# Sample residual tiles: high and low input halves side by side in one 512-column product

## The reference, cut to what matters

```python
x = x + y.astype(x.dtype)                      # y = mixer output @ ev_w_out or od_w_out
x = x + cross_attention(h, m, ...)             # ends in o @ x_w_o
x = x + (jnp.square(jax.nn.relu(h @ p['mlp_w1'][layer])) @ p['mlp_w2'][layer]).astype(x.dtype)
```

## Time and profile before

| | |
|---|---|
| Median of three runs | 2537.8 us (2537.19 to 2540.1) |
| The profiled execution: its own time, its span | 2539.81 us, 2538.0 us |
| PE busy | 2443.0 us, 96% of the span |
| DVE busy | 1531.7 us, 60% |
| ACT busy | 1150.5 us, 45% |
| Mean granted PE clock | 0.986 of full speed |

### The profile page before, as it was taken

The page is one execution under the profiler, slowest core; times in us unless marked ns, Lnnn a source line. Parts: engine busy times, 40 slices in busy tenths (PEclk is TensorE's granted clock), DMA queues, the critical chain, the costliest instruction groups (busy, mean ns, idle before and its releaser), DMA issues.

```text
span 2538.0 us, 35247 instructions
## 1 busy us (share of the span) xinstructions
PE 2443.0 (96%) x14102; PEld 2075.0 (82%) x14102; DVE 1531.7 (60%) x2599; ACT 1150.5 (45%) x2010; POOL 0.2 (0%) x4
## 2 busy tenths in 40 slices
PE   7997799899999999999999999999999999999999
PEld 4887576778888999899778888778788888888887
DVE  8988756767546755564565446656886645533332
ACT  4232336344433555544454444445665443423422
POOL 0000000000000000000000000000000000000000
PEclk9998899999999999999999999999999999999999
DMA  5324532255312455444224323223334423433332
GB/s 189 95 67 103 167 111 96 80 169 191 108 59 85 156 183 184 123 132 136 78 73 157 116 81 119 75 84 101 92 92 142 132 73 88 141 99 100 92 100 91
DMA packets 109667, 289.24 MB, mean 114 GB/s; under 512 B 18913, under 2 KB 41569, under 8 KB 108225
## 3 DMA queue, kind: packets, MB, share of 16 engines
q1 hardware_dynamic: 101392, 261.36, 33.5%
q10 hardware_dynamic: 8112, 25.63, 3.1%
HBM read 265.35 MB, written 19.50 MB: 112 GB/s over the span
## 4 chain that ended last, share of the span: by engine, by line
PE 81%; DVE 12%; ACT 4%; issue 2%; DMA 1%; SPq 0%; ACTq 0%; DVEq 0%
PE ps L1414 65%; PE ps L1504 2%; PE ps L338 2%; PE ps L1479 2%; PE ps L334 2%; DVE wlo L1391 1%; PE ps L1522 1%; PE ps L1546 1%; DVE ps L1697 1%; DVE ps L1696 1%; DVE yP L1698 1%; ACT yP L1565 1%; DMA wraw<-wt 1%; DVE x L555 1%; PE ps L1446 1%
## 5 line engine op out<-in xcount | busy, mean ns | idle before, releaser
L1414 PE MATMUL ps<-in_hP,whi 128*128 128x512 f32 x1336 | 541.1, 405 | 1.6 <-issue 1.6
L1386 ACT ACTIVATE whi<-wraw 128x1024 fp32r<-128x1024 f32 x430 | 452.2, 1053 | 194.1 <-PE ps L1414 128.7
L1391 DVE TENSOR_TENSOR wlo<-wraw,whi 128x1024 fp32r<-128x1024 f32 x431 | 523.4, 1218 | 22.7 <-ACT whi L1386 22.4
L1414 PE MATMUL ps<-in_hP,wlo 128*128 128x512 f32 x1336 | 522.9, 391 | 0.0
L1414 PE MATMUL ps<-in_lP,whi 128*128 128x512 f32 x1336 | 522.1, 391 | 0.0
L1414 PE MATMUL ps<-in_hS,whi 128*128 128x256 f32 x1088 | 320.0, 294 | 5.6 <-DVE x L1719 4.3
L1414 PE MATMUL ps<-in_lS,whi 128*128 128x256 f32 x1088 | 309.4, 284 | 0.0
L1414 PE MATMUL ps<-in_hS,wlo 128*128 128x256 f32 x1088 | 309.3, 284 | 0.0
L1414 PEld LDWEIGHTS ps<-in_hP,whi 128*128 128x128 f32 x1336 | 252.4, 189 | 63.1 <-issue 11.0
L1414 PEld LDWEIGHTS ps<-in_lP,whi 128*128 128x128 f32 x1336 | 252.3, 189 | 55.5 <-issue 5.0
L1414 PEld LDWEIGHTS ps<-in_hP,wlo 128*128 128x128 f32 x1336 | 251.9, 189 | 54.2
(11 more groups left out here) (471 smaller groups left out, 3685.7 us busy)
## 6 DMA issues: line engine op xcount, KB each, us to landing
wraw<-wt SPq DMA_DIRECT2D x432, 512.0 KB, 3.5
wraw<-wt ACTq DMA_DIRECT2D x17, 512.0 KB, 4.1
k_scratch<-region_P SPq DMA_DIRECT2D x16, 256.0 KB, 3.1
v_scratch<-vtmp SPq DMA_DIRECT2D x32, 128.0 KB, 3.0
x<-x_in SPq DMA_DIRECT2D x4, 768.0 KB, 6.8
mix_u<-x SPq DMA_DIRECT2D x32, 64.0 KB, 3.4
mix_mem<-mem_in ACTq DMA_DIRECT2D x4, 512.0 KB, 6.5
x<-x_in ACTq DMA_DIRECT2D x1, 2048.0 KB, 12.7
```

Of the source, the lines that this page charges most:

```text
L1386: nc.scalar.activation(whi[:, (n + 3) % NHI, :, :], wraw[:, ws(n), :, :], ACT.Copy).then_inc(wh.sem, 1)
L1391: nc.vector.tensor_tensor(wlo[:, ws(n), :, :], wraw[:, ws(n), :, :], whi[:, (n + 3) % NHI, :, :].bitcast(F32), ALU.subtract).then_inc(wr.s ...
L1414: last = nc.tensor.matmul(ps[:, m % 2, 0:N[prod.g]], w_[:, k, :], x_[:, k, :], start=(k == 0 and j == 0), stop=(k == KT - 1 and j == 2))
```

## The change

For residual tiles of the sample alone the high and low halves of the input are laid side by side in memory (`hid_S`, `in_S`), as `[high 256 | low 256]` for each k. One matmul of 512 columns under w_h makes w_h·x_h in columns 0 to 255 of the bank and w_h·x_l in columns 256 to 511. The product w_l·x_h stays at 256 columns and adds to the first half. So a tile has 16 matmuls and 16 weight loads where it had 24. The two halves of the bank are then added to `x` one after the other, by two DVE instructions with a `dve_chain` between them. Prompt tiles and the sample's other products are as they were.

```diff
-                hid_h[g] = sb(f"hid_h{g}", [P, KT, N[g]], F32R, on=over)
-                hid_l[g] = sb(f"hid_l{g}", [P, KT, N[g]], F32R, on=over)
+                if g == "S":
+                    hid_S = sb("hid_S", [P, KT, 2, TS], F32R, on=over)
+                    hid_h[g], hid_l[g] = hid_S[:, :, 0, :], hid_S[:, :, 1, :]
...
+            in_S = sb("in_S", [P, KT, 2, TS], F32R, on=fl)
...
+                    self.pair = None if (kind, g) != ("res", "S") else in_S if rhs is None else hid_S
...
                     if i == 0 and prod.ready is not None:
                         pe.wait_ge(*prod.ready(k))
+                    if prod.pair is not None:
+                        both = prod.pair[:, k, :, :].rearrange("p z n -> p (z n)")
+                        if k < KT - 1:
+                            nc.tensor.matmul(ps[:, m % 2, :], w_h[:, k, :], both, start=(k == 0), stop=False)
+                        last = nc.tensor.matmul(ps[:, m % 2, 0:TS], w_l[:, k, :], h_[:, k, :], start=False, stop=False)
+                        if k == KT - 1:
+                            last = nc.tensor.matmul(ps[:, m % 2, :], w_h[:, k, :], both, start=False, stop=True)
+                        continue
...
                     v.wait_ge(td.sem, m + 1)
+                    if prod.pair is not None:
+                        dve_chain(nc.vector.tensor_tensor(x[:, i, cols(g)], ps[:, b, TS:2 * TS], x[:, i, cols(g)], ALU.add))
                     nc.vector.tensor_tensor(x[:, i, cols(g)], ps[:, b, 0:N[g]], x[:, i, cols(g)], ALU.add).then_inc(tf[b].sem, 1)
```

More of the change, by code:

```diff
@@ L918, in trunk_tail @@
                 over = ExitStack()
-                hid_h[g] = sb(f"hid_h{g}", [P, KT, N[g]], F32R, on=over)
-                hid_l[g] = sb(f"hid_l{g}", [P, KT, N[g]], F32R, on=over)
+                if g == "S":
+                    hid_S = sb("hid_S", [P, KT, 2, TS], F32R, on=over)
+                    hid_h[g], hid_l[g] = hid_S[:, :, 0, :], hid_S[:, :, 1, :]
+                else:
+                    hid_h[g] = sb(f"hid_h{g}", [P, KT, N[g]], F32R, on=over)
+                    hid_l[g] = sb(f"hid_l{g}", [P, KT, N[g]], F32R, on=over)
                 over.close()
@@ L926, in trunk_tail @@
             over.close()
-            in_h = {"P": in_hP, "S": sb("in_hS", [P, KT, TS], F32R, on=fl)}
-            in_l = {"P": in_lP, "S": sb("in_lS", [P, KT, TS], F32R, on=fl)}
+            in_S = sb("in_S", [P, KT, 2, TS], F32R, on=fl)
+            in_h = {"P": in_hP, "S": in_S[:, :, 0, :]}
+            in_l = {"P": in_lP, "S": in_S[:, :, 1, :]}
             ring = {g: sb(f"ring{g}", [P, 2, N[g]], on=fl) for g in "PS"}
@@ L1111, in __init__ @@
                     self.kind, self.g, self.w0, self.ready, self.n, self.layer = "mem", "P", WT[f"kv{layer}"], ready, 2 * KT, layer
-                    self.rhs, self.norm, self.up = (in_h["P"], in_l["P"]), None, None
+                    self.rhs, self.norm, self.up, self.pair = (in_h["P"], in_l["P"]), None, None, None
                     self.sq, self.kad, self.ksc = z["sqd"].take(KT), z["kad"].take(XH), z["ksc"].take(XH)
```

## The result

The changed kernel takes 2542.5 us in the median of nine runs (2540.6 to 2548.1), the kernel before 2538.1 us in nine runs on the same chip (2535.2 to 2540.1). The ratio is 1.0022, with a 95% interval of 1.0012 to 1.0032: about 5.6 us slower, between 3.0 and 8.1 (the two medians themselves are 4.4 us apart). It is a small loss, and the interval doesn't reach down to 1.

The account below looks back on a forecast made before the run. PE bounds the kernel with 81% of the chain, DVE leading in short stretches; -4.5 + 2.15 + 2.15 + 2.7 + 0.3 + 0 = +2.8, rounded to +2.7, on 2537.8 gives 2540.5 us, range 2534.5 to 2546.

Parts of the forecast that it names:

- if a mixed pair of matmuls takes anything but 0.347 us: Sign that the prediction is wrong: a 512- and a 256-column matmul together should take 0.227 and 0.120 us.
- the other: Sign that the prediction is wrong: attention rounds of 23.1 us grow or shrink by over 0.3 us.
- The price of the second add: On DVE, each sample tile's second add costs 0.47 us, between 0.34 and about 0.6; 45 us in total.
- The rival of 0.34 us: Second add costs only 0.34 us on DVE: paced stretches cost 4.9 in all, total +0.4, 2538.2 us; chance 0.09.
- 5 x 0.47 - 0.2: Cross output of layer 1: five second adds paid in full, less two shorter tiles, +2.15 us; last 8 tiles the same.
- the second adds of tiles 0 and 1 lie in the wait for it: Cross output of layer 1: the first two tiles' second adds are hidden while DVE's statistic is awaited.
- I take the middle: On PE, a sample tile shortens by 0.106 us to 2.774 us, between bounds of no saving and 0.21 us.
- if the missing fixed part came back at the change of width: Bound on PE's gain: the sample tile would stay at 2.88 us; as a rival 2545 us, chance 0.08.
- Cross output of layer 0: Beside the prompt's cross attention DVE has 1.41 us in each slot, so 8 x 0.106 = 0.85 us is gained.
- Attention output of layer 1: Eight tiles with room on DVE but a late weight tile: an estimated gain of 0.3 us.
- Attention of MLP 1: 16 tiles beside the differential attention: DVE becomes full, PE's gain is lost, net 0, between -1.7 and +7.5 us.
- the rival of broken margins: DVE's thin cover in MLP 0 and the attention rounds fails: +5 to +10, 2543 to 2548 us; chance 0.17.

Follow-up runs that it names:

- e2: The kernel before with its matmuls kept, but each sample residual tile's add made in two chained DVE instructions; 2546.4 us, ratio 1.0031.
- e4: The changed kernel with the paired form only where DVE has room (64 tiles), the paced stretches and mixer output as before; 2537.4 us, ratio 0.9995.
- e3: The changed kernel without its first add, so the input's low part is left out of x; 2533.2 us, ratio 0.9980.
- e5: The changed kernel with matmuls grouped by width in each sample tile, two changes of width instead of fifteen; 2545.0 us, ratio 1.0026.
- e9: e7 with matmuls grouped by width in every covered tile but the first of a product; 2534.6 us, ratio 0.9986.
- e11: e9 with the first sample tile of the cross output of layer 0 back in the form of before; 2534.9 us, ratio 0.9986.
- e1: The changed kernel run again with no edit; 2544.8 us, ratio 1.0024.
- e7: e4 with the 2 MB key and value load moved behind the attention output tiles; 2535.1 us, ratio 0.9986.
- e6: The changed kernel with the 2 MB key and value load moved behind the attention output tiles; 2544.0 us, ratio 1.0022.

## Why the prediction came out as it did

2540.5 us was forecast and 2542.5 measured, inside the range of 2534.5 to 2546. But the loss was 5.6 us where 2.7 was forecast, just above the 0.2% from which the prediction calls a kernel slower, and it gave that a chance of 0.25. The mechanism was right: a second add that is paid in full where DVE leads and is hidden in MLP 0. Of the sizes below, four were missed towards the loss and one towards the gain. That the time still lies in the range is partly luck: the range's upper end was drawn for tiles that don't shorten at all, not for the two places that cost more than forecast. By one of its own signs the prediction is wrong: "if a mixed pair of matmuls takes anything but 0.347 us", and it took 0.352. By the other it isn't: the attention rounds shrank by 0.1 us.

- **The price of the second add**, 0.47 us, is 0.45 to 0.46 from start to start and 0.45 to 0.46 a slot. The last two stretches of MLP 1 cost what the working gave: +2.70 for +2.7, +2.18 for +2.15. e2 shows that it is the add and e4 that without it nothing stays. The rival of 0.34 us is out.
- **Cross output of layer 1: +2.53 for +2.15.** The form "5 x 0.47 - 0.2" was right in its first term, 5 x 0.46 = 2.3. e2, which has the adds and no shorter tile, gave +2.70, so another 0.4 us is paid. The step of the working that fails is "the second adds of tiles 0 and 1 lie in the wait for it". ACT squares the new `x` of tile 1, so it waits for the second add, and the statistic's own work on ACT (`yP`) stands behind the square. Here the changed kernel, and then the kernel before, where the square was done in time and `yP` starts as PE's two matmuls of the statistic end (1553.10 + 1.02 = 1554.12):

```profile
1553.07 0.42 DVE L1735 TENSOR_TENSOR x<-ps,x 128x256 f32<-128x256 f32 x1
1553.53 0.42 ACT L1587 ACTIVATE ringS<-x 128x256 f32<-128x256 f32 x1 [1.13 <-DVE x L1735]
1553.85 0.67 ACT L1579 ACTIVATE yP<-ps,par 128x512 f32<-128x512 f32 x1
1555.22 0.70 DVE L1710 SCALAR_TENSOR_TENSOR ps<-ps,yP 128x512 f32<-128x512 f32 x1 [1.72 <-ACT yP L1580]
...
1553.10 1.02 PE L1459 MATMUL ps<-accP,par 128*128 128x512 f32 x2
1554.16 0.69 ACT L1565 ACTIVATE yP<-ps,par 128x512 f32<-128x512 f32 x1
1555.55 0.70 DVE L1696 SCALAR_TENSOR_TENSOR ps<-ps,yP 128x512 f32<-128x512 f32 x1 [1.83 <-ACT yP L1566]
```

DVE's statistic starts 8.20 us behind the stretch's first matmul before, 8.56 us in e2 and 8.44 us in the changed kernel. 0.36 + 5 x 0.46 = 2.66 us is e2's +2.70, and 0.24 + 2.3 = 2.54 the changed kernel's +2.53. PE waited 1.81 us there instead of 0.85. The shorter tiles gave 0.12 us of the 0.2 (also in e3).
- **What a tile gains: 0.064 us, not 0.106.** This was the step "I take the middle" with the bound "if the missing fixed part came back at the change of width". It came back in part. Steps from a 512-column matmul to the next were 0.235 us and from a 256-column one 0.117, a pair 0.352 where 0.347 was forecast. e5 and e9 give some 0.026 us a tile back with fewer changes of width; the remaining 0.016 us lies in the first 512-column matmuls behind the narrow ones, whose steps are longer than the prompt's (e5). On 32 tiles of MLP 0 the miss is 1.4 us.
- **Cross output of layer 0: 0 instead of -0.85.** The working looked at the idle time of DVE in each slot and not at who waits for what stands behind the add. One of the eight adds delays `ringP`, which PE waits for (e11): 0.46 us of the 0.51 that eight tiles give. (0 is the value at an equal clock, from e1 and e7.)
- **Attention output of layer 1: +1.2 to +3.3 instead of -0.3.** Rows 14 had the late weight tile, and the working named it, but put down a gain of 0.3 us and no cost. The reserve behind it was used up, by the second adds as well as by the shorter tiles (e2 +1.01, e3 +0.29): DVE's wait grew from 2.67 to 4.20 us, PE waited and the clock fell. e6 and e7 gave the gain back by moving the load. One execution loses 1.2 us there and another 3.3, for the latter's wait is 0.5 us longer and followed by the lower clock. Why the load held the tile up longer, and why the clock fell once and not the other time, stays open.
- **Attention of MLP 1: -0.41 for 0**, so the rounds kept some 40% of the tiles' gain (16 x 0.064 = 1.0). DVE showed no idle time before the scores in those slots, as forecast, and PE waited there no longer than 0.42 us where it had been 0.34. This is where the rival of broken margins expected the loss, and it didn't come. That margins broke at the three places above, with the tile's smaller gain, is what made the loss twice the forecast.
- **Mixer output**: +0.50 and +0.39 for +0.3; its tile 5 started 0.6 us late as the working had it, with 0.28 us of idle time shown before it.

The Trainium skill, TensorE: Matmul & The Clock Gate, section "Wait — 56ns, not 53.3ns?", has about 2.5 ns fixed per warm matmul. The gain lies between that figure and the 13.2 ns of the prediction's sum: taking away eight of 24 matmuls gave 64 ns, 8 ns each, and 11 ns each grouped (2.88 - 2.79 = 0.09 us). The Trainium skill, VectorE: DVE Perf Modes, section "The DRAIN you can't avoid", says that a semaphore after each instruction costs nothing extra, by which the second add would have been the 0.34 us of rows 8; the slots grew by 0.45, so the trace doesn't agree.

The best version is e9: pair only where DVE has room, width changed twice a tile, the 2 MB load behind the tiles. It is 0.14% faster than the kernel before (0.05 to 0.23), some 3.5 us. e7 and e11 measure the same.

## What to carry to other kernels

Before a matmul saving is paid for with an instruction on a second engine, sort the tiles by who paces them where they lie, and make the change only in the ones that the matmul engine paces: here 32 of 96 tiles are the difference between e6, 0.22% slower than before, and e7, 0.14% faster. In the covered ones, the idle time ahead of the new instruction is no proof of cover; look at who waits for the work behind it, on the other engines too: one second add of 0.46 us reached PE through `ringP`, another through ACT's square. And look once more at any transfer that the trace already shows late, because both the shorter tiles and the added instructions live on its reserve.

## What the runs showed of the hardware

- Matmuls of two widths in turn cost more than each in its own stream: 0.352 us for a pair of 512 and 256 columns, against 0.2268 + 0.120 = 0.347 from the pure streams. Put in groups, the same sixteen matmuls take 2.79 instead of 2.82 us, and the steps of the 512-column ones fall from 0.236 to 0.227 us over the first five of a tile (e5).
- PE's wait of 2 us for a late weight tile was followed by a granted clock of 0.66 in the next 5 us of the view, so such a stall can cost nearly twice its length; the wait of 1.50 us at the same place in e1 was followed by 1.00. The wait of 1.57 us for `ringP` was followed by 0.67 in one execution of the changed kernel and by 1.00 in another. The fall of 745 to 755 us in the kernel before moved its stretch by 1.7 us, and that is why differences of a microsecond are read here from stretches of equal clock.
- A lower clock where DVE leads cost nothing: in the cross output of layer 1 the granted clock was 0.72 from 1560 to 1565 us in the changed kernel and 1.00 in e6, and the stretch grew by 2.53 and 2.54 us.
- Two 256-column instructions on DVE of which the second waits for the first start 0.46 us apart; one that doesn't wait starts 0.34 us behind (1560.27 to 1560.61 in the changed kernel).
